# Matrix inversion by doubling on one core: order of adds, turns, copies and gate tiles within a level

## The reference, cut to what matters

```python
def step(state, inp):
    r_t, w_t, k_t, v_t, kk_t, a_t = inp
    sa = jnp.einsum('bhvk,bhk->bhv', state, -kk_t)
    state = (state * w_t[:, :, None, :]
             + sa[..., None] * (kk_t * a_t)[:, :, None, :]
             + v_t[..., None] * k_t[:, :, None, :])
    y_t = jnp.einsum('bhvk,bhk->bhv', state, r_t)
    return state, y_t
```

## Time and profile before

| | |
|---|---|
| median of 3 runs | 2439.82 us |
| profiled execution | 2440.57 us |
| its span, first to last instruction | 2438.7 us |
| TensorE busy | 2415.1 us (99%) |
| VectorE busy | 1611.2 us (66%) |
| ScalarE busy | 1201.0 us (49%) |
| GpSimd busy | 114.4 us (5%) |
| TensorE clock granted | 0.999 |

### The profile page before, as it was taken

The page is one execution under the profiler, slowest core; times in us unless marked ns, Lnnn a source line. Parts: engine busy times, 40 slices in busy tenths (PEclk is TensorE's granted clock), DMA queues, the critical chain, the costliest instruction groups (busy, mean ns, idle before and its releaser), DMA issues.

```text
span 2438.7 us, 50836 instructions
## 1 busy us (share of the span) xinstructions
PE 2415.1 (99%) x21762; PEld 2366.8 (97%) x21762; DVE 1611.2 (66%) x1912; ACT 1201.0 (49%) x1688; POOL 114.4 (5%) x68
## 2 busy tenths in 40 slices
PE   8999999999999999999999999999999999999999
PEld 8999999999999999999999999999999999999987
DVE  6666677748566498586576545587666666666684
ACT  5444445545344484464455334554444444444564
POOL 0000000002600002002100000000000000000000
PEclk9999999999999999999999999999999999999999
DMA  6444434344555564252444555455555555555543
GB/s 240 157 158 162 161 139 158 137 179 167 188 183 182 189 235 157 106 190 89 157 155 153 219 186 188 173 195 185 181 185 189 189 187 181 184 187 189 207 173 138
DMA packets 59092, 425.57 MB, mean 175 GB/s; under 512 B 6576, under 2 KB 6704, under 8 KB 8400
## 3 DMA queue, kind: packets, MB, share of 16 engines
q1 hardware_dynamic: 58464, 421.68, 48.3%
q0 software_dynamic: 496, 1.90, 0.3%
HBM read 419.23 MB, written 4.33 MB: 174 GB/s over the span
## 4 chain that ended last, share of the span: by engine, by line
PE 94%; DVE 3%; ACT 1%; DMA 1%; issue 0%; DVEq 0%; SPq 0%; ACTq 0%
PE banks L244 27%; PE banks L246 27%; PE banks L245 27%; PE banks L298 2%; PE banks L300 1%; PE banks L299 1%; PE banks L2376 1%; PE banks L2378 1%; PE banks L2377 1%; DVE weights_lo_sb L207 1%; PE banks L573 1%; PE banks L760 1%; PE banks L776 0%; DMA raw_weights_sb<-weights 0%; PE banks L1470 0%
## 5 line engine op out<-in xcount | busy, mean ns | idle before, releaser
L244 PE MATMUL banks<-xa_hi_sb,weights_hi_sb 128*128 128x256 f32 (+3 forms) x4290 | 1219.4, 284 | 11.2 <-DVE xa_lo_sb L337 9.9
L246 PE MATMUL banks<-xa_hi_sb,weights_lo_sb 128*128 128x256 f32 (+3 forms) x4290 | 1209.7, 282 | 0.0
L245 PE MATMUL banks<-xa_lo_sb,weights_hi_sb 128*128 128x256 f32 (+3 forms) x4290 | 1207.8, 282 | 0.0
L207 DVE TENSOR_TENSOR weights_lo_sb<-raw_weights_sb,weights_hi_sb 128x1024 fp32r<-128x1024 f32 x786 | 935.5, 1234 | 259.5 <-ACT weights_hi_sb L186 254.0
L186 ACT CAST weights_hi_sb<-raw_weights_sb 128x1024 fp32r<-128x1024 f32 x786 | 779.9, 1047 | 558.5 <-DMA raw_weights_sb<-weights 557.9
L244 PEld LDWEIGHTS banks<-xa_hi_sb,weights_hi_sb 128*128 128x128 f32 x4290 | 807.1, 188 | 14.9 <-issue 12.2
L245 PEld LDWEIGHTS banks<-xa_lo_sb,weights_hi_sb 128*128 128x128 f32 x4290 | 809.8, 189 | 0.2
L246 PEld LDWEIGHTS banks<-xa_hi_sb,weights_lo_sb 128*128 128x128 f32 x4290 | 808.1, 188 | 0.0
L244 PE MATMUL banks<-xb_hi_sb,weights_hi_sb 128*128 128x256 f32 (+1 forms) x688 | 196.6, 286 | 0.6 <-DVE o_sb L1042 0.3
L246 PE MATMUL banks<-xb_hi_sb,weights_lo_sb 128*128 128x256 f32 (+1 forms) x688 | 195.0, 283 | 0.0
L245 PE MATMUL banks<-xb_lo_sb,weights_hi_sb 128*128 128x256 f32 (+1 forms) x688 | 194.8, 283 | 0.0
(11 more groups left out here) (462 smaller groups left out, 2273.6 us busy)
## 6 DMA issues: line engine op xcount, KB each, us to landing
raw_weights_sb<-weights SPq DMA_DIRECT2D x393, 1024.0 KB, 4.8
h_sb<-h SPq DMA_DIRECT2D x4, 544.0 KB, 8.7
h_aside<-h_sb SPq DMA_DIRECT2D x1, 2176.0 KB, 9.6
h_sb<-h_aside SPq DMA_DIRECT2D x1, 2176.0 KB, 9.4
out<-y_sb SPq DMA_DIRECT2D x4, 512.0 KB, 2.7
conv_gate_sb<-ple_gain POOLq DMA_DIRECT2D x1, 512.0 KB, 5.0
conv_value_sb<-ple_gain POOLq DMA_DIRECT2D x1, 512.0 KB, 7.9
masks_sb<-consts_rw POOLq DMA_DIRECT2D x1, 448.0 KB, 5.8
```

The source lines that it names most:

```text
L207: dve.tensor_tensor(c.w_lo[n % RAW][:, half], c.raw[n % RAW][:, half], c.w_hi[n % RAW][:, half].bitcast(F32), ALU.subtract).then_inc(c.sem ...
L244: pe.matmul(out, w_hi[:, k, a], x_hi[:, tile, cols], start=begin, stop=False)
L245: pe.matmul(out, w_hi[:, k, a], x_lo[:, tile, cols], start=False, stop=False)
L246: done = pe.matmul(out, w_lo[:, k, a], x_hi[:, tile, cols], start=False, stop=end)
```

## The change

It does three things within each level of the inversion. VectorE does the adds of both halves first, then both turns. ScalarE copies T of a half before it makes the moves of that half. TensorE does one gate tile more between the T products and the update (5 instead of 4), and one fewer between the update and the next T products (1 instead of 2; 2 instead of 3).

```diff
@@ rw_pe
                 m.then_inc(S("tm_done"), 1)
-            kept_products(c, pe, 4)
+            kept_products(c, pe, 5)
             for p in range(2):
                 pe.wait_ge(S("turn_ready"), v + p + 1)
                 pe.wait_ge(S("cross_ready"), v + p + 1)
...
                 m.then_inc(S("inverse_done"), 1)
-            kept_products(c, pe, 3 if level in (3, 5) else 2)
+            kept_products(c, pe, 2 if level in (3, 5) else 1)
@@ rw_act
                 v = 2 * (5 * b + level - 1) + g + 1
+                act.wait_ge(S("tm_done"), v)
+                act.copy(t["tt"][:, 8 * g:8 * g + 8, :].rearrange("p (k u) i -> p k (u i)", k=2),
+                         ps[:, 2 * g:2 * g + 2, 0:256]).then_inc(S("t_ready"), 1)
                 act.wait_ge(S("turn_ready"), v)
...
                 m.then_inc(S("cross_ready"), 1)
-                act.wait_ge(S("tm_done"), v)
-                act.copy(t["tt"][:, 8 * g:8 * g + 8, :].rearrange("p (k u) i -> p k (u i)", k=2),
-                         ps[:, 2 * g:2 * g + 2, 0:256]).then_inc(S("t_ready"), 1)
@@ rw_dve
                                   ALU.add).then_inc(S("inverse_ready"), 1)
-                dve.wait_ge(S("inverse_ready"), v)
+            for p in range(2):
+                dve.wait_ge(S("inverse_ready"), 2 * (5 * b + level - 1) + p + 1)
                 if level < 5:
                     turn(p)
```

## The result

The changed kernel takes 2451.01 us (median of 6 runs, 2446.74 to 2452.57), the one before it on the same chip 2440.03 (6 runs, 2439.49 to 2441.2): a ratio of 1.0043, 95% interval 1.0032 to 1.0054. It is slower by 11 us. The forecast was 2443.6, with a range up to 2445.1. The changed kernel spreads more from run to run (5.8 us, against 1.7 before), and rows exist of one execution only.

What follows compares the result with a forecast made beforehand. TensorE was taken as the bound, busy 99% of the span. Per half, -1.02 + 0.75 + 1.91 + 0.17 + 0.10 = +1.91, twice +3.8 us, gave 2443.6 us; range 2438.9 to 2445.1.

Steps and rivals of the forecast that it cites:

- Part 1: TensorE's gate tiles in the inversion levels: regrouped with none added, slots and weight loads staying in place; cost nothing.
- Part 2: ScalarE's T copies before moves: second updates wait a new 0.13 us at each level; 0.75 per half in sum.
- Part 3: VectorE's adds before turns: second add in time, old stall before the T products gone; -1.02 us per half.
- Part 4: GpSimd's mask product starts 0.18 us before VectorE's weight difference and delays it; TensorE stalls cost 1.91 per half.
- Rival A: Lock between GpSimd and VectorE does not bite in the inversion: twice -0.3 us, 2439.5; chance 0.18.
- rival C: Lock as forecast, with VectorE adds 0.70 apart and a ScalarE signal of 0.25: 2444.7 to 2445.4; chance 0.09.
- Part 5: Inversion exit: TensorE waits for level 5's second add before the transposes; 0.10 us per half.

Runs made afterwards that it cites:

- load_later: Changed kernel with one weight load per half held until the last add of level 5; 2444.16 us, ratio 1.0014.
- gate_only: Kernel before with gate tiles 5 and 1 alone, VectorE and ScalarE as before; 2444.16 us, ratio 1.0015.
- hold: Kernel before with TensorE held in front of the T products of level 5 until the second turn of level 4 is done; 2445.37 us, ratio 1.0022.
- t_on_vector: Changed kernel with GpSimd's mask product in halves, second copy of T on VectorE, 4 and 3 gate tiles in level 5; 2450.69 us, ratio 1.0043.
- adds_gate: Changed kernel with ScalarE's order as before (moves, T, moves, T); 2445.5 us, ratio 1.0021.
- adds_only: Kernel before with both adds in front of both turns alone; 2441.83 us, ratio 1.0005.
- mask_halves: Changed kernel with GpSimd's mask product in two halves, each behind its own half of the T products; 2442.97 us, ratio 1.0006.
- hold_later: Kernel before with the same TensorE wait as hold, and the level 5 weight load held until the last add; 2444.15 us, ratio 1.0018.
- before_later: Kernel before with the weight load of level 5 held alone; 2441.02 us, ratio 1.0000.
- halves_later: Changed kernel with GpSimd's mask product in halves and the load of level 5 held; 2441.72 us, ratio 1.0004.

## Why the prediction was wrong, point by point

**Part 1, gate tiles: the step that failed.** It says that "slots, weight loads and gate takes stay where they were. Cost nothing", and the sum adds that "loads follow its own signals". The load of level 5 does stay where it was: it goes out 0.46 behind the start of the last gate matmul in front of the T block, in the kernel before (matmul 981.26, load 981.72) as in after (981.96, 982.42). What moved is the T block. The stall of the lock, 0.62, stands between that matmul and the block, so the load is now issued 0.37 in front of the block and no longer 0.25 behind it; and TensorE's instruction fetch comes behind the block (by 1.01 and 1.27 in load_later, which has the same TensorE program). It finds a load that is 1.4 to 1.6 old and starts 4.3 behind the load's issue. Cost 2.3 + 2.0 in two gaps and 1.3 to 1.6 at the lower clock behind the second. The prediction had the stall (0.66) and gave it no effect but its own length. It is the stall and not the count of tiles: gate_only has the 5 and 1 tiles and its load 0.25 behind the block, hold has the 4 and 2 with a wait put in that place.

Load and fetch of level 5 in the runs, half by half, us:

| kernel, half | load issued in front of (+) or behind (-) the T block of level 5 | fetch started behind the issue | gap |
|---|---|---|---|
| after, 1 and 2 | +0.37, +0.37 | 4.3, 4.3 | 2.4, 2.1 |
| hold, 2 | +1.42 | 4.5 | 2.0 |
| t_on_vector, 2 | +0.15 | 4.4 | 3.0 |
| adds_gate, 1 and 2 | -0.03, -0.04 | 0.97, 1.12 | none |
| before 2, adds_only, gate_only, mask_halves, t_on_vector 1 | -0.25 | 0.16 to 0.91 | none |
| load_later, 1 | -5.5 | before it | none |

The first three rows are of fetches that were due later than those of the others. When, can only be worked out, from a run or a half of the same order in which no load held it back: 1.4 to 1.6 behind the issue in after (from load_later), 1.3 in t_on_vector (from its own first half), 2.3 in hold (from hold_later). They started at 4.3 to 4.5, when the load (4.8 from issue to landing) was nearly done. So a border lies between 1.12 and some 1.3 if it is one in time; what it is, no run tells.

The whole trace of after has the same two groups: of its 111 packets of queue 8, 85 start with a weight load under way, 16 of them up to 0.9 behind its issue, 63 from 4.1 to 4.8 behind it and 6 elsewhere. The kernel before has them too (61 of 83 at 4.0 to 4.9). So a fetch that waits for a load is common and mostly costs nothing. In the weight stages the packets stand mostly 12 to 19 us apart. In the inversion, where the matmuls are short, they stand 3.5 to 5.5 apart, and a delay of 3 us is more than TensorE has in hand.

**Part 2, T in front of the moves**: right, and a little short. The steps came at 0.76, 1.37, 2.21 and 2.82. The block of updates is longer by 0.22 in levels 1 and 2 and by 0.17 in levels 3 and 4 (0.18 and 0.13 forecast).

**Part 3, both adds first**: right. Blocks of 1.16 to 1.21, but for one of 1.28 (level 5 of the second half), turns within 0.1 of the forecast places, adds 0.60 to 0.68 apart (0.61).

**Part 4, the lock**: right, and within 0.06. First by 0.12 (forecast 0.18), difference until 1.08 behind GpSimd, stalls 0.58, 0.60 and 0.62 (0.60, 0.65, 0.66). Rival A is out, and rival C's adds and signal did not come. adds_only shows the other side of the same switch, with VectorE first by 0.08. The rule of the Trainium skill ("SBUF — State Buffer", section "SBUF: two separate sides") held in these pairs. The other rule that the prediction cites from the Trainium skill ("VectorE: DVE Perf Modes", section "The DRAIN you can't avoid") would have had the adds as far apart as linked ones, 0.70 to 0.72; they were 0.60 to 0.68 apart. The margin of 0.12 was narrow: adds_only, 0.08 the other way, has no stall by the lock, so that this side came out in after was partly luck.

**Part 5 and the sum**: the exit came as forecast (transposes 2.18 behind the first update in load_later, 2.1 forecast). The sum was +3.8 for the whole, and load_later, in which only the failed step is mended, has +4.0 in the two inversions, +3.2 in span and +3.65 in the medians (2444.16 against 2440.51). So the reasons of the costed terms were right, and what was missing was a term that I had put at nothing without a cover named for it.

**The range** ended at 2445.1, since every bound in it was a bound on a costed term. A term at zero had no bound. The chance of "slower by over 0.2%" was 0.14, for rival C, and it came from elsewhere.

## What to carry to other kernels

A load that is released by a mark in the busiest engine's list, and a stall of that engine right behind the mark, drift apart from what the engine does next. Put the engine's instruction fetch beside the loads, as one more transfer with a due time: find it in the queue called instruction, and keep large loads from being issued shortly before it is due. It matters where instructions are short and packets follow each other closely, here every 4 to 5 us. And when two engines share a lock, read which of them starts first and by how much: here 0.1 us decides over 2 us of the one or the other, and whatever shortens the stage ahead can turn it round.

## What the runs showed of the hardware

- **Instruction fetch behind a load.** Packets of 16 KB, mostly 0.9 to 1.4 long, one for some 260 TensorE instructions. Behind a 1 MB load they start either at once (up to 1.1 after its issue) or mostly 4.1 to 4.8 after it, and where TensorE had run dry it resumed 1.4 to 1.5 after the packet's end. The Trainium skill's page "Runtime: NRT & Kernel Launch" (section "Instruction fetch mechanics") has the 16 KB blocks and calls the cost of crossing from one to the next mostly hidden. This case agrees with both: of the 63 late packets in after, the two of level 5 cost a gap, of 2.4 and 2.1.
- **The clock behind a gap.** After 2.1 us (after, second half) and 3.0 us (t_on_vector, second half) without a matmul, TensorE ran for 3.4 us at 1.2 GHz; after 2.4 us (after, first half) it did not. Elsewhere the same: at 891 us all 13 profiled executions have a stop of 2.1 to 3.0, and the lower clock followed in three of them (hold, hold_later, adds_gate), behind stops of 2.1, and not behind those of 2.8 and 3.0 (before_later, halves_later). So the length of the stop does not decide it, and the 1.3 to 1.6 us that it costs in after need not be in each execution. What else it takes was not found.
- **The lock is decided by 0.1 us**: VectorE first by 0.08, 1.18 for it and 3.33 for GpSimd; GpSimd first by 0.12, 2.41 for it and 3.37 for VectorE.
